# A two-block diffusion transformer on one core: delta-rule outputs one step later, narrow solve tiles, and state-space tables beside both attentions

## The reference

```
first block   layer 0: MLA attention (8 heads, full softmax), layer norm, SwiGLU, layer norm
              layer 1: gated delta rule (16 value heads, both directions), layer norm, SwiGLU, layer norm
second block  layer 0: windowed attention with a sink (16 heads), output product, layer norm
              layer 1: S5 state-space mixer with GLU, output product, layer norm
```

```
def step(S, inp):
    w_i, u_i, qd_i, kd_i, a_i, gl_i = inp
    v_new = u_i - w_i @ S
    o_i = qd_i @ S + a_i @ v_new
    S = S * gl_i + kd_i.T @ v_new
    return S, o_i
```

## Time and profile before

| | us |
|---|---|
| median of 3 runs | 4598.3 (4596.3 to 4599.4) |
| profiled execution | 4582.04 |
| its span, first to last instruction | 4580.3 |

### The profile page before, as it was taken

One profiled execution on the slowest core, in us unless ns is written; L12 is line 12 of the kernel. 1 busy time (PEld: TensorE's weight loads), 2 busy tenths in 40 slices (PEclk: granted clock), 3 DMA queues, 4 the chain that ended last, 5 costly groups with the idle time before them and its releaser, 6 DMA issues. The chain is left out here.

```text
span 4580.3 us, 51208 instructions
## 1 busy us (share of the span) xinstructions
PE 4024.1 (88%) x18484; PEld 2931.4 (64%) x18484; DVE 2674.5 (58%) x4686; ACT 1154.4 (25%) x2590; POOL 1473.2 (32%) x1602
## 2 busy tenths in 40 slices
PE   7899899999898668888999978989989687667998
PEld 4577455555455557777878864568755365566886
DVE  6635799832588854347578744255686329903353
ACT  3133211100222744442021102126310222141012
POOL 1143499700000488200000390046789300350000
PEclk9999999999899879989999989999999898778999
DMA  4501465521110464325345551100255344783222
GB/s 180 170 19 56 124 188 179 170 91 44 64 56 34 146 172 94 75 53 180 106 152 173 158 168 65 60 21 1 68 150 146 124 156 158 256 230 130 83 77 70
DMA packets 291080, 532.42 MB, mean 116 GB/s; under 512 B 181040, under 2 KB 187696, under 8 KB 266544
## 3 DMA queue, kind: packets, MB, share of 16 engines
q1 hardware_dynamic: 237488, 348.70, 24.3%
q0 software_dynamic: 53088, 180.65, 13.0%
q10 hardware_dynamic: 288, 0.32, 0.0%
HBM read 429.42 MB, written 100.01 MB: 116 GB/s over the span
## 5 line engine op out<-in xcount | busy, mean ns | idle before, releaser
L409 PE MATMUL P<-hu,ring 128*128 128x384 f32 (+1 forms) x2448 | 745.1, 458 | 20.2 <-PEq L171 12.0
L409 PEld LDWEIGHTS P<-hu,ring 128*128 128x128 f32 x2448 | 466.3, 191 | 274.6 <-issue 22.2
L646 PE MATMUL P<-area,ring 128*128 128x256 f32 (+1 forms) x1880 | 491.2, 417 | 54.6 <-PEq L385 24.5
L646 PEld LDWEIGHTS P<-area,ring 128*128 128x128 f32 x1880 | 361.0, 193 | 174.1 <-issue 69.3
L409 PE MATMUL P<-area,ring 128*128 128x256 f32 (+1 forms) x1584 | 443.2, 432 | 4.7 <-DVE area L537 2.8
L409 PEld LDWEIGHTS P<-area,ring 128*128 128x128 f32 x1584 | 301.6, 191 | 129.1 <-issue 4.8
L646 PE MATMUL P<-area,hu 128*128 128x256 f32 (+1 forms) x1104 | 297.0, 423 | 1.1 <-DVE hu L735 1.1
L646 PEld LDWEIGHTS P<-area,hu 128*128 128x128 f32 x1104 | 209.5, 190 | 78.9 <-DVE hu L735 2.1
L866 POOL TENSOR_TENSOR fold<-mod,vec 128x16 f32<-128x16 f32 (+1 forms) x5 | 1.0, 206 | 778.7 <-SPq L845 771.6
L2022 POOL TENSOR_TENSOR area<-area 128x512 f32<-128x512 f32 (+2 forms) x128 | 235.9, 1843 | 10.0
L2416 DVE SCALAR_TENSOR_TENSOR area<-area 128x1024 f32<-128x1024 f32 x122 | 203.5, 1668 | 18.5 <-ACT area L2492 16.4
(11 more groups left out here) (417 smaller groups left out, 7486.1 us busy)
## 6 DMA issues: line engine op xcount, KB each, us to landing
ring<-in_w_ffn_in SPq DMA_DIRECT2D x44, 1024.0 KB, 4.9
ring<-s_c POOLq DMA_DIRECT2D x32, 1152.0 KB, 6.3
area<-in_w_mod SPq DMA_DIRECT2D x69, 512.0 KB, 3.6
stat<-in_w_mod SPq DMA_DIRECT2D x39, 512.0 KB, 3.6
s_c<-area POOLq DMA_DIRECT2D x32, 576.0 KB, 3.4
ring<-in_w_ffn_out SPq DMA_DIRECT2D x24, 704.0 KB, 4.2
area<-s_fa POOLq DMA_DIRECT2D x64, 256.0 KB, 6.6
area<-in_s_bn POOLq DMA_DIRECT2D x64, 256.0 KB, 7.4
```

Source lines behind the costliest of these rows:

```text
L409: last = mm(to, col(a, k), b[:, k, :], start=fresh and k == 0, stop=k == q - 1, skip_group_check=True)
L646: last = mm(to, a[:, 128 * k:128 * k + 128], b[k], start=fresh and k == 0, stop=k == q - 1, skip_group_check=True)
```

## The change

- In both attentions the scaling of the probabilities goes from GpSimd to ScalarE (`weigh`, in place, after the exponential of the next unit). GpSimd makes S5 tables there instead. The sum with the sink becomes a one-operand form.
- The 16 blocks of tables now lie beside the first attention (3), `ffn_in0` (8) and the windowed attention (5). `ffn_out1`, `att_z` and `att_out` have none.
- In the second pass of `gdn_heads` both parts of the output are added by VectorE one step later (`outputs(n - 1)`, between R and the update of S), from PSUM places of their own. TensorE takes values and queries of one direction, then of the other, with the growth of S between.
- The solve writes into one bank. `blocks32`, the first part of `blocks64` and `cross64` use the long operand in column slices of 32 or 64, one matmul for each slice, and `whole` and the second part of `blocks64` alternate between column groups. `outward` goes through one bank in two halves, before and behind the values of s=3.
- Attention tiles have four places instead of two and are loaded three steps ahead; `diag_load(0)`, `fin_load(1)`, `diag_load(1)` and the first turned keys are loaded earlier, in the first pass.
- A masked product on VectorE in the first pass becomes two one-operand instructions.

```diff
-            for n in range(U):
-
-                pool.wait_ge(sem["inv"], n + 1)
-                p = prob[n % slots][:, 0:width(n)]
-                nc.gpsimd.tensor_scalar(p, p, small[:, n % slots, 6:7], None, ALU.mult).then_inc(sem["unit"], 1)
+            pool_work(pool)
...
+            def weigh(n):
+
+                act.wait_ge(sem["inv"], n + 1)
+                p = prob[n % slots][:, 0:width(n)]
+                nc.scalar.activation(p, p, ACT.Copy, scale=small[:, n % slots, 6:7]).then_inc(sem["unit"], 1)
...
+                if 1 <= n <= U:
+                    weigh(n - 1)
...
-                    nc.vector.tensor_tensor(total, small[:, n % slots, 2:3], small[:, n % slots, 3:4], ALU.add).then_inc(sem["total"], 1)
+                    nc.vector.tensor_scalar(total, small[:, n % slots, 2:3], small[:, n % slots, 3:4], None, ALU.add).then_inc(sem["total"], 1)
...
+    AT_in = AT[0:2] + GT[0:2]
...
-    PA, PB, PC = ([bank(2 * k + d) for d in range(2)] for k in range(3))
-    places = lambda hh: (bank(6), bank(7)) if hh else (bank(0), bank(1))
+    PA, PB = ([bank(2 * k + d) for d in range(2)] for k in range(2))
+    PQ = lambda m, d: bank(4 + m % 2, 256, 256 * d)
+    PO = lambda d: bank(6, 256, 256 * d)
+    place = lambda hh: bank(7) if hh else bank(0)
...
+            def load_kt(i):
+
+                if i >= 2:
+                    sp.wait_ge(sn, per5(i - 2, 4, 1))
+                else:
+                    sp.wait_ge(kt_out[i], 16 * 4)
+                sp.dma_start(flat(KT[i % 2]), c.gdn["kt"][i]).then_inc(kt_in[i % 2], 16)
+
+            def load_at(m):
+
+                if m >= 4:
+                    sp.wait_ge(av, 2 * (m - 3))
+                else:
+                    sp.wait_ge(at_out[m], 16 * 8)
+                    if m >= 2:
+                        sp.wait_ge(dd, 48)
+                sp.dma_start(AT_in[m % 4].rearrange("p d v n -> p (d v n)"), c.gdn["at"][m // 4, m % 4]).then_inc(at_in[m % 4], 16)
...
+                if n == 47:
+                    for m in range(3):
+                        load_at(m)
...
                 if (i, s) == (5, 1):
                     sp.wait_ge(zeroed, 1)
                     fin_load(0)
+                elif (i, s) == (5, 4):
+                    diag_load(0)
                 elif (i, s) == (6, 1):
-                    diag_load(0)
-                elif (i, s) == (7, 1):
                     fin_load(1)
-            for n in range(4):
-                sp.wait_ge(at_out[n], 16 * 8)
-            for n in range(2):
-                sp.wait_ge(kt_out[n], 16 * 4)
-
-            def load_kt(i):
-
-                if i >= 2:
-                    sp.wait_ge(sn, per5(i - 2, 4, 1))
-                sp.dma_start(flat(KT[i % 2]), c.gdn["kt"][i]).then_inc(kt_in[i % 2], 16)
-
-            def load_at(m):
-
-                if m >= 2:
-                    sp.wait_ge(av, 2 * (m - 1))
-                sp.dma_start(AT[m % 2].rearrange("p d v n -> p (d v n)"), c.gdn["at"][m // 4, m % 4]).then_inc(at_in[m % 2], 16)
-            load_kt(0)
-            load_at(0)
-            load_at(1)
+                elif (i, s) == (6, 4):
+                    diag_load(1)
+                elif (i, s) == (7, 3):
+                    load_kt(0)
...
-                if s % 3 == 0 and hh + 1 < 16:
+                if s % 3 == 0 and 1 <= hh < 15:
                     diag_load(hh + 1)
-                if s >= 2 and 4 * i + s < 32:
-                    load_at(4 * i + s)
+                if s >= 2 and 4 * i + s + 1 < 32:
+                    load_at(4 * i + s + 1)
...
-                    last = mm(F0[:, 32 * k:32 * k + 32], near[n][:, k, :], x_lead[n][:, k, :], start=True, stop=True)
+                    for b in range(4):
+                        to = of32(b)
+                        last = mm(F[to, 32 * k:32 * k + 32], near[n][:, k, to], x_lead[n][:, k, :], start=True, stop=True)
...
-                    last = mm(F0[:, 64 * k:64 * k + 64], far[n][:, k, :], X5[n][:, k, :], start=True, stop=True)
+                    for to in (hi, lo):
+                        last = mm(F[to, 64 * k:64 * k + 64], far[n][:, k, to], X5[n][:, k, :], start=True, stop=True)
...
-                for d, (of, to) in enumerate(((hi, lo), (lo, hi))):
-                    for k in range(6):
-                        last = mm(F1[to, 64 * k:64 * k + 64], V6[:, d, k, :], six(x[:, d])[:, k, of], start=True, stop=True)
+                for k in range(6):
+                    for d, (of, to) in enumerate(((hi, lo), (lo, hi))):
+                        last = mm(F[to, 64 * k:64 * k + 64], V6[:, d, k, :], six(x[:, d])[:, k, of], start=True, stop=True)
...
-            def outward(i):
+            def outward(i, v):
 
                 pe.wait_ge(unit, i + 1)
-                for v, to in enumerate((bank(6), bank(7))):
-                    for t in range(4):
-                        last = nc.tensor.transpose(to[:, 128 * t:128 * t + 128], o_sum[i % 2][:, t, v, :], c.ident[:, :])
+                pe.wait_ge(kept_o, 2 * i + v)
+                for t in range(4):
+                    last = nc.tensor.transpose(bank(7, 128, 128 * t), o_sum[i % 2][:, t, v, :], c.ident[:, :])
...
+                if s == 0:
+                    pe.wait_ge(kt_in[i % 2], 16 * (i // 2 + 1))
+                values(n, 0)
                 if s >= 2:
+                    asked(n, 0)
+                values(n, 1)
                 if s < 5:
+                    grow(n, 0)
+                if s >= 2:
+                    asked(n, 1)
+                if s < 5:
+                    grow(n, 1)
                 if s >= 2:
                     m = 4 * i + s - 2
+                    pe.wait_ge(at_in[m % 4], 16 * (m // 4 + 1))
+                    if m:
+                        pe.wait_ge(oav, 2 * m)
                     for d in range(2):
                         pe.wait_ge(vc, per4(i, s - 2, d))
                         for v in range(2):
+                            last = mm(PO(d)[:, 128 * v:128 * v + 128], AT_in[m % 4][:, d, v, :], VN[:, d, v, :], start=True, stop=True)
                         last.then_inc(av, 1)
+                if s == 3 and i:
+                    outward(i - 1, 1)
...
+            def outputs(n):
+
+                i, s = order[n]
+                m = 4 * i + s - 2
+                dve.wait_ge(qs, per4(i, s - 2, 1))
+                for d in range(2):
+                    t = chunk[d][s]
+                    if s == 2 and d == 0 and i >= 2:
+                        dve.wait_ge(turn_o, 2 * (i - 1))
+                    if s >= 4:
+                        dve.wait_ge(oav, per4(i, s - 3, 1))
+                    for v in range(2):
+                        src, to = PQ(m, d)[:, 128 * v:128 * v + 128], o_sum[i % 2][:, t, v, :]
+                        if s < 4:
+                            last = V.tensor_scalar(to, src, col(i, 2, s, d, v), None, ALU.mult)
+                        else:
+                            last = stt(out=to, in0=src, scalar=col(i, 2, s, d, v), in1=to, op0=ALU.mult, op1=ALU.add)
+                    last.then_inc(oq, 1)
+                dve.wait_ge(av, per4(i, s - 2, 1))
+                for d in range(2):
+                    dve.wait_ge(oq, per4(i, s - 2, d))
+                    to = o_sum[i % 2][:, chunk[d][s]]
+                    tt(to, to, pair(PO(d)), ALU.add).then_inc(oav, 1)
...
+                if n and order[n - 1][1] >= 2:
+                    outputs(n - 1)
...
-                tt(GT[n % 3][:, 1], tri[:, 1:2, :].broadcast_to([128, 2, 128]),
-                   vcols(i, 5, s, 1).unsqueeze(2).broadcast_to([128, 2, 128]), ALU.mult).then_inc(gtd, 1)
+                for v in range(2):
+                    last = V.tensor_scalar(GT[n % 3][:, 1, v, :], tri[:, 1, :], col(i, 5, s, 1, v), None, ALU.mult)
+                last.then_inc(gtd, 1)
...
+              pool_work=lambda pool: s5_tables(c, pool, [cut(flat_u, T, 1, 5376)[:, 0, :], area(16 * T, 3 * T), flat_stat[:, T:2 * T]], 0, 3))
+                 (lambda pool: s5_tables(c, pool, [area(KF * T, 7840)], 3, 11), None),
-    feed_forward(1, (0,), LATS, hidden, (None, lambda pool: s5_tables(c, pool, KF * T, 7, 10)),
+              pool_work=lambda pool: s5_tables(c, pool, [area(21120, 7840)], 11, 16))
-                pool=lambda pool: s5_tables(c, pool, 16 * T, 10, 13))
-             pool=lambda pool: s5_tables(c, pool, 16 * T, 13, 16))
```

More of the change, by code:

```diff
@@ L1572, in blocks64 @@
                 for k in range(6):
[L1573 to L1577 removed]
+                    for b in range(4):
+                        to = of32(b)
+                        mm(F[to, 32 * k:32 * k + 32], V5[:, k, to], x_tail[n][:, k, :], start=True, stop=True)
@@ L1978, in s5_scratch, with s5_tables, take @@
             "h": dram("s5_h", 128, KD * LAT), "u": dram("s5_u", 128, KD * LAT)}
-def s5_tables(c, pool, at, first, end):
+def s5_tables(c, pool, spaces, first, end):
     nc = c.nc
-    take = lambda *shape: (c.view(place[0], *shape), place.__setitem__(0, place[0] + int(np.prod(shape))))[0]
-    place = [at]
```

(8 more changed lines are left out.)

151 lines of the change are left out of this document (63 added, 88 removed).

## The result

Before: 4598.9 us median of 4 runs (4596.3 to 4615.6) taken beside 4 runs of the changed kernel, **4489.3 us** (4482.4 to 4493.0). Ratio 0.9753, 95% interval 0.9726 to 0.9779: faster by 109.5 us. The forecast was 4532, its range 4508 to 4562. The profiled execution of the changed kernel took 4482.4 us (4480.6 of span); against the 4580.3 of before that is 99.7 us.

What follows compares the result with a forecast made beforehand. It looked past TensorE's 88% busy mean to its idle time at stage boundaries and in the delta rule's second pass. Terms -40 + 13 + 7 - 46 = -66 took the median of 4598.3 to 4532 us, range 4508 to 4562.

Steps and rivals of the forecast that it cites:

- tables out of `ffn_out1`, `att_z`, `att_out`: Three stages where GpSimd's late table stores hold up what follows; freeing them was to give -40 us, bounds -34 and -43.
- eighth block beside `ffn_in0`: One more table block makes `ffn_out0` wait for GpSimd until 945 to 949: +13 us, bounds +9 and +17.
- tables beside the attentions: Three blocks beside the first attention and five beside the windowed one fit at GpSimd's quiet pace: 0 us.
- ScalarE's scaling, windowed attention: Scaling delays ScalarE's copies, so flips wait at two units of six in each of 16 heads: +7 us, bounds -6 and +12.
- delta rule, the pieces of 48: Second pass, solve: `blocks32` and half of `blocks64`, as 48 narrow instructions at 35 ns, take 1.7 us: +0.35 each.
- 48 also overlap: Second pass, solve: the favourable bound, -18 us, should the 48 narrow instructions overlap too.
- DMA waits -18: Second pass: `blocks32`'s seven waits for `fin_load`, 18.2 us, vanish because its loads start some 8 us sooner: -18 us.
- pieces -11: Second pass: the new solve pieces, over 15 halves, give -11 us, bounds +4 and -18.
- The wait at s=3: Second pass: L1657 waits there for R behind output work on VectorE; later outputs save 0.6 us each, -5 us.
- The term of -3.5: Second pass: `blocks32` waits 0.49 us for ScalarE's copy of the turned output; copying half earlier saves 3.5 us.
- The drain rival: Some 45 narrow instruction groups drain TensorE; at 1.5 us a group, +67 us cancels all gains. Chance 0.03.
- the rival that the rule gains its DMA waits only: Delta rule: solve pieces get no faster and VectorE's outputs delay S, giving -18 instead of -46: 4560 us. Chance 0.11.

Runs made afterwards that it cites:

- 1: The changed kernel with the whole delta rule (`gdn_heads`, both passes) as before: 4576.0 us, ratio 0.9949 to the kernel before.
- 3: The changed kernel with all solve pieces as before, its loads, banks and late outputs kept: 4540.2 us, ratio 0.9877 to the kernel before.
- wide32: The changed kernel with the two 48-instruction pieces back at 12 wide instructions each, 64-row pieces still narrow: 4520.7 us, ratio 0.983 to the kernel before.
- 8: The kernel before with only the scaling of the probabilities moved from GpSimd to ScalarE, in both attentions: 4604.7 us, ratio 1.002.

## Why the prediction was wrong in size

Step by step; what a profile gives is a shift of a stage, what an experiment gives a difference of medians.

| step | forecast | measured |
|---|---|---|
| tables out of `ffn_out1`, `att_z`, `att_out` | -40 (-25.5, -4.9, -9.7; bounds -34 to -43) | -46 (shifts -27.5, -8.5, -10.5); the way back +47 |
| eighth block beside `ffn_in0` | +13 | +11 to +13 (means of 5 and 8 profiles); taking it out -18 |
| tables beside the attentions | 0 | 0 (235.4 against 235.6) |
| ScalarE's scaling, windowed attention | +7 | +6.7; alone +7 |
| delta rule, all but the pieces | -35 | -36 (1 and 3); stage -38 |
| delta rule, `cross64`, `whole` (measured with the second half of `blocks64`) | -17 | -20 (wide32 against all wide); stage -28 |
| **delta rule, the pieces of 48** | **+5** (with the row above -11, +4 to -18) | **-31** (wide32); stage -23, starts -25 |

The last column adds up to some -115 us where the medians say -109.5, within the scatter. The miss of 43 us is for the most part the last row: 28 to 36 us, by stage or by medians.

**The step that failed** is the price of the narrow pieces: "`blocks32` and half of `blocks64` become 48 narrow instructions at the 35 ns of L1577 (0.84 / 24): 1.7, so +0.35". Measured: 0.63 us. The row it took, L1577, is one of one column group at a time. Just ahead of it I had written of `whole` that it takes all of one direction first, and of L2234 that it alternates and is cheaper; then I priced the 48, which alternate between four groups, by a row that doesn't. My bound for "48 also overlap", -18, allows each of them 0.23 us less (7 us over 30 pieces), so 1.47: dearer still than the same instructions group by group (1.41), where alternating saves nothing. In TensorE's busy time a half was to go from 6.8 us (3 x 1.52 + 1.43 + 0.84) to 6.1. Measured over 16 halves it went from 7.2 (115.2) to 3.7 (58.7): the wide ones were 0.4 dearer than their rows (some run at the lower clock, where one takes 2.5 to 2.8), the narrow ones 2.4 cheaper. The second half of `blocks64`, which also alternates now, had no term: 14.0 us for all halves became 9.3.

**The terms were not independent.** I summed "DMA waits -18" and "pieces -11". The run with the pieces alone shows that the wait of 18 us would have grown to 39 without the early loads, and the late loads cost 32 in the changed kernel. Given loads that are early enough, nearly every microsecond off TensorE's pieces is one off the pair: 56.5 of busy time, 51 of the stage.

**Where the sum was right by luck.** The delta rule without the pieces was to give 35 us and gave 36, but not by the forecast's terms. In the stage, from the rule of before to the same kernel with the wide pieces (1 and 3), TensorE's idle time falls by 23 us (68.9 to 45.8), where the waits of the forecast, less its 1.5 us at the end, make 29. Its busy time falls by 15 (327.1 to 312.2, at a clock of 0.94 in place of 0.88), where the forecast has 6. The load wait went from 19.6 us to nothing, but 7.5 us for the copy of `whole` stand in its place, for which there was no term. The wait at s=3 went from 15.0 to 6.3, more than the forecast's 5. The term of -3.5 was a slip: half of 0.49 us in each pair is 2 at the most, and all of the waits for that copy are 2.9. `att_z` is another case where the place was wrong: the forecast had 3.9 us at its boundary and 1 for VectorE, and more of the 8.5 lies inside the stage.

**What held.** The end of the tables' overhang behind `ffn_out1` and `att_out`: 5.95 and 8.15 us of idle time where some 7 to 9 were foreseen. GpSimd's pace beside an attention: 43.4 us a block in the first one ((380.1 - 293.4) / 2, from the second row below: durations, then first and last start), 43.9 in the windowed one, where the last store is issued at 3175.4, nine microseconds before TensorE ends.

```profile
L2106 POOL DMA_DIRECT2D s_fb<-area x13: 605/621/621, 586.9 to 3175.4; - x13
L2106 POOL DMA_DIRECT2D s_fb<-stat x3: 605/621/621, 293.4 to 380.1; - x3
```

`ffn_out0` waits for GpSimd, of whose eighth block the last store is at 942.29 (forecast 942.1). The first growth of S comes 2.7 us sooner relative to the first pass (shift +19.2 where the work on `gdn_q` begins, +16.5 here), forecast 4. The wait of `cross64` stays. The drain rival is out: `blocks32` and `blocks64` stand between wide groups with idle time only where a load or a copy is awaited, and the narrow forms are faster in each pair of kernels. So is the rival that the rule gains its DMA waits only.

**What stays open.** Late outputs cost 14 us when undone, where the forecast's terms for them (-5 and -3.5) make 8.5; the rows name the normalisation and R but the runs don't part them. Half of the 20 us in the stage is not idle time at all: TensorE's busy time there is 263.7 us in place of 254.3, at a clock of 0.95 in place of 0.98. The first attention is as long as before, 175.3 and 175.4 us from its first score to `mla_out`; it ends 2.5 us later (415.4 to 418.0) because it starts later. In the windowed attention the second wait of each head was not found (8).

## What to carry to other kernels

Before pricing small matmuls from a row, look at which partitions their outputs go to, one after the other: the same instructions cost 29, 18 or 13 ns here, by order alone. When a wait and a piece of work on the path are shortened together, don't add their gains: ask what the wait would be with the work already gone (18 became 39 here). And where GpSimd gets work beside a stage that ends in a barrier, it must end first: a last store nine microseconds ahead of TensorE's end cost nothing, one eight behind it (422.0 against 414.3) cost fifteen (15.6 us of idle time in place of 0.65). Work for GpSimd costs inside a stage too, where VectorE is near the path (`att_z`).

## What the runs showed of the hardware

Narrow instructions in the order of four column groups cost 13 ns each, under half of the same instructions group by group (0.63 and 1.41 us for 48); group by group, 48 cost about what 12 wide ones do (1.52). I had expected neither. VectorE's 92 instructions in `att_z` take twice as long beside GpSimd's tables as without them (129 to 133 us against 63). And the start of a stage scatters from one profiled execution to the next: `ffn_out0` starts at 932.2 and 937.7 in two kernels that are the same up to there (before, and the pieces alone), and at 931.9 to 939.5 in the five with seven blocks. From the layer norm behind `att_out` to the start of `s5_out`, work that no experiment touches, the profiles take 858.1 to 876.6 us. That is as much as one of the terms or more: such a term is better read from several profiles than from a pair.
